# Two down projections, 16 groups of eight block products against 16 groups of seven

## The reference, cut to what matters

```python
def conv_glu(hn, w_up, conv_w, conv_b, w_down):
    up = hn @ w_up
    gate, val = jnp.split(up, 2, axis=-1)
    gate = dwconv_centred(gate, conv_w, conv_b)
    return (jax.nn.gelu(gate, approximate=True) * val) @ w_down     # (256 x 5632) @ (5632 x 2048)
...
    ff = conv_glu(hn, w_ffn_up[i], ffn_conv_w[i], ffn_conv_b[i], w_ffn_down[i])
    h = h + rmsnorm(ff, ffn_norm_post[i])
    gate = jax.nn.sigmoid(rmsnorm(h, ple_norm_pre[i]) @ w_ple_gate[i])
    h = h + rmsnorm(gate * (p[i] @ w_ple[i]), ple_norm_post[i])
```

## Time and profile before

| | |
|---|---|
| median of 3 runs | 2378.72 us (2378.43 to 2379.81) |
| profiled execution | 2378.37 us, of it 2376.6 us from the first to the last instruction |
| granted TensorE clock | 0.999 of full speed |
| TensorE busy | 2361.9 us, 11890 matmuls |
| DVE, ACT, POOL busy | 1522.0, 1195.6, 266.2 us |

### The profile page before, as it was taken

The page is one execution under the profiler, slowest core; times in us unless marked ns, Lnnn a source line. Parts: engine busy times, 40 slices in busy tenths (PEclk is TensorE's granted clock), DMA queues, the critical chain, the costliest instruction groups (busy, mean ns, idle before and its releaser), DMA issues.

```text
span 2376.6 us, 29824 instructions
## 1 busy us (share of the span) xinstructions
PE 2361.9 (99%) x11890; PEld 1982.9 (83%) x11890; DVE 1522.0 (64%) x1965; ACT 1195.6 (50%) x1613; POOL 266.2 (11%) x250
## 2 busy tenths in 40 slices
PE   9999999999999999999999999999999999999999
PEld 7878898888888888888788888887888888888887
DVE  7898577675467775575755556657665554656556
ACT  7876454444444444465655555535444444444442
POOL 1262013321013221000000000001000000000000
PEclk9999999999999999999999999999999999999999
DMA  8446656656665666565566565565665666556653
GB/s 297 156 145 198 215 176 195 188 191 192 193 193 187 188 193 207 191 203 175 176 185 205 158 196 162 167 190 164 191 181 180 214 192 197 177 182 182 189 177 125
DMA packets 122940, 444.04 MB, mean 187 GB/s; under 512 B 13744, under 2 KB 15408, under 8 KB 122288
## 3 DMA queue, kind: packets, MB, share of 16 engines
q1 hardware_dynamic: 122800, 442.12, 59.6%
HBM read 439.97 MB, written 2.10 MB: 186 GB/s over the span
## 4 chain that ended last, share of the span: by engine, by line
PE 93%; DVE 4%; ACT 2%; DMA 1%; issue 1%; SPq 0%; DVEq 0%; ACTq 0%
PE bank L702 92%; DVE wlo L1505 1%; DMA raw<-in_w 1%; DVE ev L1508 1%; ACT whi L1054 1%; PE bank L793 0%; DVE hT L1508 0%; DVE hn L1508 0%; PE bank L978 0%; PE bank L1045 0%; DVE xa L1508 0%; ACT hT L1222 0%; PE bank L1000 0%; DMA hT<-in_xT 0%; ACT L1228 0%
## 5 line engine op out<-in xcount | busy, mean ns | idle before, releaser
L1505 DVE TENSOR_TENSOR wlo<-raw,whi 128x1024 fp32r<-128x1024 f32 (+2 forms) x811 | 1012.9, 1252 | 771.2 <-ACT whi L1054 769.2
L1054 ACT ACTIVATE whi<-raw 128x1024 fp32r<-128x1024 f32 (+1 forms) x813 | 854.7, 1054 | 958.9 <-PE bank L702 942.4
L702 PE MATMUL bank<-xa,whi 128*128 128x512 f32 (+1 forms) x2688 | 841.5, 395 | 6.9 <-DVE xa L1508 3.5
L702 PE MATMUL bank<-whi,xa 128*128 128x512 f32 x2048 | 639.4, 393 | 2.2 <-DVE wlo L1505 1.8
L702 PEld LDWEIGHTS bank<-xa,wlo 128*128 128x128 f32 x2656 | 497.5, 188 | 115.0
L702 PE MATMUL bank<-xa,wlo 128*128 128x256 f32 (+1 forms) x2656 | 520.9, 278 | 0.0
L702 PE MATMUL bank<-whi,xb 128*128 128x512 f32 x1536 | 473.8, 390 | 0.0
L702 PEld LDWEIGHTS bank<-whi,xa 128*128 128x128 f32 x2048 | 379.7, 188 | 82.6 <-issue 4.7
L702 PEld LDWEIGHTS bank<-xa,whi 128*128 128x128 f32 x2688 | 411.0, 188 | 16.1 <-issue 6.6
L702 PE MATMUL bank<-wlo,xa 128*128 128x512 f32 x1024 | 399.1, 390 | 0.0
L702 PEld LDWEIGHTS bank<-whi,xb 128*128 128x128 f32 x1536 | 287.3, 188 | 59.3 <-DVE wlo L1505 0.3
(11 more groups left out here) (244 smaller groups left out, 1264.5 us busy)
## 6 DMA issues: line engine op xcount, KB each, us to landing
raw<-in_w SPq DMA_DIRECT2D x803, 512.0 KB, 3.8
hT<-in_ln_rows SPq DMA_DIRECT2D x2, 2048.0 KB, 8.3
raw<-in_w SPq DMA_DIRECT2D x9, 256.0 KB, 2.8
X<-in_post SPq DMA_DIRECT2D x3, 768.0 KB, 5.5
S<-in_x SPq DMA_DIRECT2D x4, 512.0 KB, 7.8
hT<-in_x SPq DMA_DIRECT2D x1, 2048.0 KB, 8.2
out<-S SPq DMA_DIRECT2D x8, 256.0 KB, 2.5
hT<-in_xT SPq DMA_DIRECT2D x3, 512.0 KB, 6.8
```

Source lines behind the costliest of these rows:

```text
L702: return pe.matmul(o, w, x, start=start, stop=stop, skip_group_check=True)
L1054: act.activation(hi, r, ACT.Copy).then_inc(*w_high(i))
L1505: return dve.tensor_tensor(o, x, y, op)
```

## The change

It regroups 8 of every 22 rows (p = 0 to 3, two rows each) of each half. For two rows and two column blocks (1024 columns) the kernel before has two pieces, eight products of a 128 x 128 token block with a 128 x 512 weight block, three matmuls each. The new form has seven products (Strassen's scheme in Winograd's variant), in four parts: `upper` (one product), `lower`, `pair_sums` and `full_sums` (two each). Four of the seven accumulate into side banks (4 to 7), three straight into tiles.

- The weights of `pair_sums` and `full_sums` are sums of quarter blocks. POOL makes them, four additions of 128 x 512 for each group (step "sums"), out of the two `raw` buffers, which stay held so long. The sum buffers exist once: the next group's sums wait for the split of this group's `full_sums`.
- The token operands of four products are sums too: step "mixed" on POOL (one addition of 128 x 512, four of 128 x 128), "mixed_high" on ACT, "mixed_low" on DVE, eight times in all. Those of p = 0 and 1 are made in the up part, those of p = 2 and 3 in the down part.
- `paired_out` replaces `natural_out`. For a pair of column blocks it issues two (`down0`) or three (`down1`) plain pieces, four groups of four parts and two plain pieces, and four or three plain pieces: 30 pieces, twice.
- The side banks are folded into the tiles (steps "fold", "fold_end"); for `down1` POOL then adds the folded values to `sn`, four additions of 128 x 512 (signal "joined"), and DVE's step "down1" waits for it. `down0` is now emptied by DVE.
- The sums, the folds, the squares and the post gain of `down1` lie in the space of `xa` (`wide`), free once the up part of half 1 is done.

```diff
-Use = namedtuple("Use", "mat col k0 n cols block first last")
+Use = namedtuple("Use", "mat col k0 n cols block first last part", defaults=("",))
+SUMS = ("pair_sums", "full_sums")
+COMBINED = (0, 1, 2, 3)
+EARLY = (0, 1)
+IN_PAIRS = (0, 1)
...
+    def paired_out(kind, operand, mat, k, start, groups, end):
+
+        begun = len(uses) - 1
+        for c in (0, 2):
+            pair = [begin(kind, c + j, operand, "natural", 512) for j in range(2)]
+            touched, left = set(), [(j, p) for j, p in start + sum([g[1:] for g in groups], ()) + end]
+
+            def plain(j, p):
+                b = pair[j]
+                left.remove((j, p))
+                first, last = j not in touched, j == 1 and (1, p) == end[-1]
+                touched.add(j)
+                use(b, mat, 512 * (c + j), k + 2 * p, 2, first, last)
+
+            def part(name, row, col, first, last=False):
+                uses.append(Use(mat, 512 * (c + col), row, 1, 1024, pair[0], first, last, name))
+                return len(uses) - 1
+
+            for piece in start:
+                plain(*piece)
+            for p, one, two in groups:
+                first, last, row = p == groups[0][0], p == groups[-1][0], k + 2 * p
+                a = part("upper", row, 0, first)
+                late(max(a - 7, begun + 2) if k else a - 7, "sums", a)
+                part("lower", row + 1, 0, first)
+                part("pair_sums", row, 0, first)
+                d = part("full_sums", row, 0, first, last)
+                plain(*one)
+                plain(*two)
+            late(d + 1, "fold", kind, c, d)
+            late(d + 2, "fold_end", kind, c)
+            late(d + 2, kind, pair[0])
+            for piece in end:
+                plain(*piece)
+            assert not left
+        return len(uses) - 1
+
+    def mix(u, half, p):
+        late(u, "mixed", half, p)
+        late(u + 2, "mixed_high", half, p)
+        late(u + 3, "mixed_low", half, p)
...
+            if half in IN_PAIRS and q in EARLY:
+                mix(e + d + 5, half, q)
         ends["up", half] = len(uses) - 1
-        ends["down", half] = natural_out(f"down{half}", ("ff",), "w_ffn_down", pairs(*range(22 * half, 22 * half + 22, 2)), 3)
+        if half in IN_PAIRS:
+            n = 2 + half
+            for i, p in enumerate(COMBINED):
+                if p not in EARLY:
+                    mix(len(uses) + n + 6 * (i - 1) - 5, half, p)
+            turns = tuple((j, p) for j in range(2) for p in range(4, 11))
+            ends["down", half] = paired_out(f"down{half}", ("ff",), "w_ffn_down", 22 * half, turns[:n],
+                                            tuple((p, turns[n + 2 * i], turns[n + 2 * i + 1]) for i, p in enumerate(COMBINED)),
+                                            turns[n + 8:])
+        else:
+            ends["down", half] = natural_out(f"down{half}", ("ff",), "w_ffn_down", pairs(*range(22 * half, 22 * half + 22, 2)), 3)
...
+                if turn >= NRAW:
+                    before = loaded[turn - NRAW]
+                    q.wait_ge(*w_low.of(before))
+                    if before < JOINED:
+                        q.wait_ge(*x_low.of("xa", 0, sum(STARTS[before]) - 1))
+                    if uses[before].part == "upper":
+                        q.wait_ge(*pool_val.of("sum", before, 2))
+                    elif uses[before].part == "lower":
+                        q.wait_ge(*pool_val.of("sum", before - 1, 4))
...
+                def product(B, x, c, start, stop=False):
+                    xh, xl = x
+                    mm(B[:, :], xh, hi[:, 512 * c:512 * c + 512], start)
+                    mm(B[:, :], xl, hi[:, 512 * c:512 * c + 512], False)
+                    return mm(B[:, :], xh, lo_[:, 512 * c:512 * c + 512], False, stop)
...
+                q.wait_ge(*w_low.of(u))
+                if s.part == "upper":
+                    m = product(bank[5], tokens(s.k0, 0), 0, side_free(5), s.last)
+                elif s.part == "lower":
+                    product(bank[n % 4], tokens(s.k0, 0), 0, begins(0))
+                    m = product(bank[(n + 2) % 4], mixture(4), 1, begins(2))
+                elif s.part == "pair_sums":
+                    product(bank[6], mixture(1), 0, side_free(6), s.last)
+                    m = product(bank[4], mixture(3), 1, side_free(4), s.last)
+                else:
+                    product(bank[7], mixture(2), 0, side_free(7), s.last)
+                    m = product(bank[(n + 1) % 4], tokens(s.k0 + 1, 1), 1, begins(1), s.last)
...
+                if uses[i].part == "pair_sums":
+                    q.wait_ge(*pool_val.of("sum", group_of(i), 2))
+                elif uses[i].part == "full_sums":
+                    q.wait_ge(*pool_val.of("sum", group_of(i), 4))
+                else:
+                    q.wait_ge(*landed(i))
...
+                    elif step == "mixed_high":
+                        half, p = k
+                        q.wait_ge(*pool_val.of("mixed", half, p, 4))
+                        if half and p not in EARLY:
+                            q.wait_ge(*piece_tile.of("used", XA_FREE[1]))
+                        elif half and 0 in IN_PAIRS:
+                            q.wait_ge(*w_low.of(LAST_SUMS))
+                        elif p not in EARLY:
+                            q.wait_ge(*x_low.of("ff", 21))
+                        act.activation(mixed_set(half, p)[:, 0, :], mixed_v, ACT.Copy).then_inc(*x_high("mixed", 11 * half + p))
+                    elif step == "fold":
+                        kind, c, d = k
+                        if kind == "down0":
+                            q.wait_ge(*vec_val.of("grown", 0, 7))
+                        elif c:
+                            q.wait_ge(*pool_val.of("joined", kind, 0))
+                            q.wait_ge(*squares.of("ss", 1, 1, 1))
+                        else:
+                            q.wait_ge(*piece_tile.of("used", XA_FREE[1]))
+                        q.wait_ge(*piece_tile.of("used", d))
+                        act.activation(folded(kind, c, 0, 0), bank[5][:, :], ACT.Copy).then_inc(*act_evac("first", kind, c))
...
+                    elif step == "fold":
+                        kind, c, d = k
+                        x = [[folded(kind, c, t, j) for j in range(2)] for t in range(2)]
+                        q.wait_ge(*act_evac.of("first", kind, c))
+                        tt(x[0][1], bank[7][:, :], x[0][0], ALU.subtract).then_inc(*vec_val("less", kind, c))
+                        q.wait_ge(*vec_val.now())
+                        tt(x[1][0], x[0][1], bank[4][:, :], ALU.add).then_inc(*vec_val("fold", kind, c, 0))
+                    elif step == "fold_end":
+                        kind, c = k
+                        x = [[folded(kind, c, t, j) for j in range(2)] for t in range(2)]
+                        q.wait_ge(*vec_val.of("fold", kind, c, 0))
+                        tt(x[0][1], x[0][1], bank[6][:, :], ALU.add).then_inc(*vec_val("fold", kind, c, 1))
+                        tt(x[1][1], x[1][0], bank[6][:, :], ALU.add).then_inc(*vec_val("folded", kind, c))
...
+                            if 1 in IN_PAIRS:
+                                q.wait_ge(*pool_val.of("joined", "down1", c - c % 2))
...
+                        r = mixed_x.rearrange("p (k t) -> p k t", k=2)
+                        tt(r, f32(x[:, :, 0:T]), f32(x[:, :, T:2 * T]), ALU.add).then_inc(*pool_val("mixed", half, p, 0))
+                        upper, lower = mixed_x[:, 0:T], mixed_x[:, T:2 * T]
+                        v = [mixed_v[:, 128 * i:128 * i + 128] for i in range(4)]
+                        q.wait_ge(*pool_val.now())
+                        tt(v[0], upper[:, 128:256], lower[:, 128:256], ALU.subtract).then_inc(*pool_val("mixed", half, p, 1))
+                        tt(v[2], upper[:, 128:256], upper[:, 0:128], ALU.subtract).then_inc(*pool_val("mixed", half, p, 3))
+                        q.wait_ge(*pool_val.of("mixed", half, p, 1))
+                        tt(v[1], upper[:, 0:128], v[0], ALU.subtract).then_inc(*pool_val("mixed", half, p, 2))
+                        q.wait_ge(*pool_val.now())
+                        tt(v[3], lower[:, 0:128], v[1], ALU.subtract).then_inc(*pool_val("mixed", half, p, 4))
...
+                        earlier = [i for i, s in enumerate(uses[:a]) if s.part == "full_sums"]
+                        if earlier:
+                            q.wait_ge(*w_low.of(earlier[-1]))
+                        if uses[a].first and uses[a].col == 0:
+                            q.wait_ge(*(x_low.of("p", 1) if uses[a].block.kind == "down0" else piece_tile.of("used", XA_FREE[1])))
...
+                        q.wait_ge(*landed(a))
+                        tt(pair[:, 0:512], up[:, 0:512], up[:, 512:1024], ALU.add).then_inc(*pool_val("sum", a, 1))
+                        q.wait_ge(*landed(a + 1))
```

(65 more changed lines are left out.)

101 lines of the change are left out of this document (87 added, 14 removed).

## The result

The changed kernel takes 2408.26 us (median of 4 runs, 2407.38 to 2409.73); the kernel before, in runs beside it, 2379.26 us (2378.43 to 2380.05). The ratio is 1.0122, with a 95% interval of 1.0110 to 1.0134: 29 us slower, 4 us above the forecast of 2404.0 and inside its range. The profiled execution took 2407.56 us, 2405.8 of it inside the span.

The account below looks back on a forecast made before the run. TensorE was taken to bound the kernel, so only removed matmuls or added TensorE waits move the time: 2378.4 - 10.9 + 10.9 + 15.4 + 2.5 + 1.5 + 6.2 = 2404.0 us, range 2375 to 2418.

Parts of the forecast that it names:

- What is saved: All 16 groups: 21 matmuls instead of 24 each, 48 fewer on TensorE, 10.9 us saved.
- The price of a pair of operations: POOL addition of 128 x 512 beside a DVE split: they take turns, 2.25 us a pair.
- The ring with a mix: Down parts, one full_sums split to the next with a mix between: 16.3 us against TensorE's 10.2; without a mix 11.9.
- The short additions: POOL's four 128 x 128 additions in a mix: 0.45 us each by a line, 2.1 for four with gaps.
- The first pairs: First column pairs of down0 and down1: TensorE waits for late full_sums splits, costing 10.9 and 15.4 us.
- The join: Behind down1's first pair: DVE's and ACT's splits queue behind the wait for POOL's four additions; 0 to 5, taken 2.5 us.
- The second pair's cycles: Down1's second column pair, now with little lead: 0 to 3 us, taken as 1.5.
- The end: End of down1: DVE reaches the last tiles 5.6 to 8.3 us later; cost 4.8 to 7.5, taken 6.2 us.
- What would show it: Trace signs: wlo waits some 25 us, transpositions about 6, additions near 2, splits near 2.2, ACT idle 5 or more.
- the one without contention: Rival: POOL and DVE contend little, cycles with a mix 11.9 us; 2376.5 us, 2374 to 2388; chance 0.15.
- the rival of late buffers: Rival: slower weight landings in bursts add 1 us at each of 12 steps; 2416 us, 2412 to 2430; chance 0.13.

Follow-up runs that it names:

- Sums that read nothing: Against the changed kernel, POOL's four additions of a group replaced by six memsets of 128x1024 with the same waits and signals: 2384.74 us, ratio 1.0020.
- The even block's step later: Against the changed kernel, down1's even-block step on DVE and ACT at the fifth and fourth piece behind the groups instead of the second: 2405.63 us, ratio 1.0114.
- The even tiles emptied ahead of the join: Against the changed kernel, in down1's first pair DVE adds even tiles to sn before POOL's join; squares and weights at the fifth piece: 2406.14 us, ratio 1.0113.
- ten groups: Against the changed kernel, ten groups instead of sixteen, with more plain pieces behind them and down1's joined-waiting step five pieces behind: 2372.36 us, ratio 0.9971.

## Why the prediction was right

The sign, the size (2404.0 against 2408.3) and the main mechanism held. By its steps:

- *What is saved*: 48 matmuls, 10.9 us. Right.
- *The price of a pair of operations*, 2.25 us. Right, by "Sums that read nothing". The ring with a mix took 15.8 us in down0 and 15.7 and 15.8 in down1 (944.84 to 960.63 for the last) against 16.3; without a mix 11.3 against 11.9. The splits of full_sums of groups 1 to 3 were ready 21.1, 36.9 and 48.1 us after the start of down0, against 21.9, 38.2 and 50.1. The short additions, which the trace of before did not show alone, take 0.46 to 0.50 each undisturbed (1.00 for two), near the 0.45 of the line, but the first two meet a split or two and take 1.74 to 2.73.
- *The first pairs*: 10.9 forecast and 9.4 measured, 15.4 and 13.0. Each error is a half us for a cycle, summed over three or four. But both measured values hold slow matmuls that the sum did not know: of the 22.4 us about 17 are waits and 5 the lower clock. The waits alone were oversized by 9 us.
- *The join*: 2.5 forecast, 5.1 measured. Here the step failed, in its cause. It asked when DVE's splits behind the join are needed; the bank that the same DVE step empties is needed first. The rows that show it are the 3.79 us ahead of 992.27; "The even block's step later" and "The even tiles emptied ahead of the join" set the two causes apart, by where TensorE waits; their times don't.
- *The second pair's cycles*: 1.5 and 1.8. Right.
- *The end*: 6.2 and 9.3. DVE came even later than forecast (5.6 to 8.3 us): it began on the last tiles at 1062.57, 9.5 us behind TensorE's end of down1 at 1053.05, where the kernel before did so 0.2 us ahead of it (1032.92 against 1033.15). And TensorE met the wait at the pieces ahead of the transpositions, for the banks, not at the transpositions. Some 3 us of the 9.3 are the lower clock.
- *What would show it*: splits and POOL additions near 2.2 and 2 (the 60 additions of the sums from 548 us on have a mean of 1.87), ACT idle 7.3 to 7.9 us ahead of the mixed copies, four times, the list of waits led by wlo. All seen, but with 16.9 us in TensorE's line instead of some 25. The transpositions with 6 us were not.
- *The rivals*: the one without contention put its ring at 11.9 us and its time at 2376.5. The kernel with that ring (12.2 us) took 2384.7. The distances between its matmuls hold 6.5 us in the first pairs, 1.7 of them the lower clock, against the rival's 4.2, but 9.2 at the join and the end, where it had 4.8: those need no contention of the sums. Of the rival of late buffers there is a trace: ACT waits for landings 47.5 us in all instead of 15.9, 3.2 at most. The weights still land in 3.8 us in the median, and none of the waits shown above ends with a landing.

The sum came within 4 us because two errors offset each other: the waits of the first pairs were 9 us too long, and 10 us of lower clock were missing (5 in the first pairs, 1.7 at the join, 3.4 at the end). That is luck: nothing in the prediction ties the two together. Without the clock the end was right (5.9) and the join 1 us short.

## What to carry to other kernels

A product saved on the bounding engine by sums on the others is gained only where the whole ring of those sums (POOL, ACT, DVE and back) is shorter than TensorE's work between two of them, or where a lead covers it; ten groups in covered places gave 7 us, sixteen lost 29. Time the ring with the stretched durations of the two engines that take turns, not with those of each alone. And where a step that frees a bank gets a new wait, ask first who needs the bank, then who is queued behind the step.

## What the runs showed of the hardware

- *Short waits cost twice.* After the waits of 3.29, 3.30, 3.79 and 4.13 us between two starts, the next matmuls came at 0.43 us, the 1.2 GHz level, for some 3 us; after the one of 2.29 us at 570 they came at 0.23 at once. The length of the last wait alone doesn't settle it. The slow pace also followed one of 1.66 us at 940.59, which had one of 1.23 shortly ahead of it (the line below), and one of 2.25 us at 1063.40. With the mix's copy three pieces later a wait of 3.19 us, up to 590.94, was followed by the quick pace, and without groups in the second pair of down1 the quick pace held for 0.8 us behind one of 3.29 before the slow one began. About 10 of 38.6 us are lost in this way.

```profile
940.90:944.30 3.40, 3.40 (x9) 2.67 (x8) 1.03 (x1) 1.07 (x2) 2.22 (x3) 0.50 0.83 261
```

- *POOL's shapes.* 128x512 takes 1.30 us alone and 2.28 in turn with a split; 128x128 takes 0.46 to 0.50 alone, 0.87 in the mean of two of which one meets a split, and up to 1.46 when it does. So a short addition that meets a split lasts as long as an undisturbed 128x512 one or longer.
- *A memset takes no turn*: six of 128x1024 in 6.0 us, beside them four splits in 4.1 us, as short as alone.
- *Freed work is not free.* Twice a step was moved so that DVE's splits could run during the join, and twice the join grew by 2.4 us.
